# Stores on SP's queue, the output weight split by GpSimd, and another order of column tiles, in a transformer kernel on one core

## The reference

```python
qa, ka, va, ga, qb, kb, vb, gb, qn, kn, vn, gn = split_proj(h @ w_in[l])
lam = (jnp.exp(jnp.sum(lambda_q1[l] * lambda_k1[l])) - jnp.exp(jnp.sum(lambda_q2[l] * lambda_k2[l]))
       + lam_init).astype(jnp.float32)
...
oa = map_query_blocks(lambda q_blk: diff_attend(q_blk, ka_all, va_all, lam), qa)
ya = (rms_norm_2(oa, diff_subln[l]) * (1 - lam_init)).reshape(b, s, A_W) * jax.nn.silu(ga)
...
yb = map_query_blocks(lambda q_blk: gqa_attend(q_blk, kb_all, vb_all), qb) * jax.nn.silu(gb)
...
yn = neighbourhood_attend(qn, kn, vn.reshape(b, s, C_HEADS, HEAD_DIM), kn_c, vn_c, nat_rpb[l], rows)
yn = yn * jax.nn.silu(gn)
y = jnp.concatenate([ya, yb, yn], axis=-1) @ w_out[l]
...
x = x + gt[:, None] * y
```

## Time and profile before

| | us |
|---|---|
| median of three runs | 4307.61 |
| lowest and highest | 4303.0, 4307.77 |
| the profiled execution | 4303.49 |
| its span in the trace | 4301.7 |
| PE busy | 3607.9 (84%) |
| DVE busy | 2565.4 (60%) |
| ACT busy | 2070.9 (48%) |
| GpSimd busy | 1025.2 (24%) |

### The profile page before, as it was taken

How to read it: one execution, slowest core, us unless ns; L and a number is a source line. 1 busy time by engine, 2 the same in 40 slices (tenths; PEclk the granted TensorE clock), 3 DMA queues, 4 the chain that set the end, 5 groups by cost and what they waited for, 6 DMA issues and landing times. The chain is left out here.

```text
span 4301.7 us, 68958 instructions
## 1 busy us (share of the span) xinstructions
PE 3607.9 (84%) x24823; PEld 2975.7 (69%) x24823; DVE 2565.4 (60%) x4482; ACT 2070.9 (48%) x3653; POOL 1025.2 (24%) x964
## 2 busy tenths in 40 slices
PE   3997699988579999589995999974979996999748
PEld 3994487766468888468884778753768875788637
DVE  1205365543677888457645777655558755777654
ACT  1315456751057777542223666654442224766542
POOL 0212100000036656225551000000025560000002
PEclk8998899998689999789997999987989997999989
DMA  7127733313969999433326324431233326244413
GB/s 274 57 85 229 211 79 79 80 38 114 362 255 390 397 396 396 155 141 111 106 76 184 73 59 92 88 64 62 67 134 110 113 79 176 61 91 91 92 47 95
DMA packets 329465, 624.68 MB, mean 145 GB/s; under 512 B 118692, under 2 KB 174916, under 8 KB 328100
## 3 DMA queue, kind: packets, MB, share of 16 engines
q1 hardware_dynamic: 290272, 502.07, 36.7%
q0 software_dynamic: 35040, 104.50, 8.0%
q10 hardware_dynamic: 3812, 13.69, 1.0%
HBM read 486.20 MB, written 133.97 MB: 144 GB/s over the span
## 5 line engine op out<-in xcount | busy, mean ns | idle before, releaser
L1207 ACT ACTIVATE aa_prob<-aa_ps,aa_nm 128x256 f32<-128x256 f32 (+2 forms) x680 | 474.1, 697 | 281.1 <-DVEq L1158 242.5
L1078 PE MATMUL aa_ps<-aa_op 128*128 128x512 f32 (+2 forms) x1408 | 376.4, 381 | 194.8 <-DVEq L1166 126.3
L1157 DVE TENSOR_REDUCE aa_nm<-aa_ps 128x1 f32<-128x1280 f32 (+1 forms) x252 | 346.1, 1373 | 200.7 <-PE aa_ps L1078 188.3
L1078 PEld LDWEIGHTS aa_ps<-aa_op 128*128 128x128 f32 x1408 | 237.2, 194 | 314.9 <-issue 156.2
L1977 PE MATMUL pr_ps<-pr_wH,hT_part 128*128 128x512 f32 (+1 forms) x1120 | 428.7, 383 | 0.0
L1729 ACT ACTIVATE ex_high<-ex_ring 128x2048 fp32r<-128x2048 f32 x192 | 368.7, 1920 | 97.9 <-PE ex_pg L1705 40.1
L1775 DVE TENSOR_TENSOR ex_ring_part<-ex_ring,ex_high 128x2048 fp32r<-128x2048 f32 x144 | 373.8, 2596 | 51.5 <-ACTq L1730 39.8
L1108 PE MATMUL aa_po<-aa_pT,aa_op 128*64 128x128 f32 x5552 | 389.9, 283 | 0.0
L1089 PE MATMUL aa_ps<-ident,aa_prob 128*128 128x128 f32 x2776 | 378.5, 280 | 6.3 <-ACTq L1211 6.2
L1977 PE MATMUL pr_ps<-pr_wH,x_sb_part 128*128 128x512 f32 x896 | 359.4, 401 | 19.9 <-DVEq L2053 19.9
L1977 PE MATMUL pr_ps<-pr_ws_part,x_sb_part 128*128 128x512 f32 x896 | 353.1, 394 | 0.0
(11 more groups left out here) (300 smaller groups left out, 7158.3 us busy)
## 6 DMA issues: line engine op xcount, KB each, us to landing
ex_ring<-in_w_gate SPq DMA_DIRECT2D x64, 1024.0 KB, 10.2
ex_ring<-in_w_up SPq DMA_DIRECT2D x64, 1024.0 KB, 8.7
ex_ring<-in_w_down SPq DMA_DIRECT2D x64, 1024.0 KB, 8.5
aa_op<-z_d SPq DMA_DIRECT2D x120, 320.0 KB, 9.4
z_d<-pr_zT POOLq DMA_DIRECT2D x120, 256.0 KB, 3.1
pr_ws<-in_w_in SPq DMA_DIRECT2D x14, 2048.0 KB, 9.1
mod_w<-in_w_ada SPq DMA_DIRECT2D x10, 2048.0 KB, 13.8
rt_mw<-in_w_ada SPq DMA_DIRECT2D x8, 2048.0 KB, 16.9
```

The source lines that it names most:

```text
L1078: mm = tensor.matmul(ps[:, base[h] + at:base[h] + at + m], q.bitcast(F32R), kk.bitcast(F32R), start=i == 0, stop=i == len(ab) - 1)
L1157: vector.tensor_reduce(most, scores[:, 0:g_.count[t]], AX.X, ALU.max, negate=True)
L1207: scalar.activation(prob[:, base[h] + c0:base[h] + c1], ps[:, base[h] + c0:base[h] + c1], ACT.Exp, bias=nm[:, h % 4:h % 4 + 1], scale=-1.0 ...
```

## The change

Six edits. (1) The attention's output stores go to SP, between its loads; `o` has six buffers instead of four. (2) `w_out` is loaded by SP after the third store; GpSimd makes both of its parts while the last unit runs: the high part goes into the operand slot that the last unit does not use (`operand_slots`), the low part to its old place. `stage_out` makes no parts any more. (3) The lambda vectors are loaded with the near heads' biases, and DVE and ACT make lambda in the attention, from slot 40 on. In `stage_out` SP loads tiles 0 and 1 first, then the gates, for which DVE waits at the third pass only. (4) The projection's stores go to SP, in step order between the weight loads. (5) The output's stores go to SP. (6) The last column tiles are 5, 4, 6 instead of 6, 4, 5: the last one, 6, has no Q or K columns, while 2 now alternates with 5, both with Q and K columns.

```diff
-COLUMN_TILES = (1, 0, 3, 2, 6, 4, 5)
+COLUMN_TILES = (1, 0, 3, 2, 5, 4, 6)
...
+    def operand_slots(held, name, groups):
+        op = held.enter_context(nc.sbuf_tensor(f"{name}_op", [P, 2, max(g_.cols for g_ in groups)], F32))
+        free = sum(g_.pairs for g_ in groups) % 2
+        return op, op[:, free, 0:KC * D].rearrange("p (k d) -> p k d", d=D)
...
+    def stage_attention(name, groups, slots_, weight, asides=(), prepare=None):
+        dv, RING, OR, PREPARE = 64, 4, 6, 40
+        op, wH = slots_
...
+                loads(0)
+                loads(1)
+                for m in range(M):
+                    for u in range(2, len(units)):
+                        if unit_end[u - 2] == m + 1:
+                            sp.wait_ge(pv, m + 1)
+                            loads(u)
+                    g_, p, t, _ = steps[2 * m]
+                    sp.wait_ge(od, m + 1)
+                    sp.dma_start(g_.addr(p)[3][t * P:(t + 1) * P, :], o[:, m % OR]).then_inc(st[m % OR], 16)
+                    if m == 0 and prepare is not None:
+                        prepare[0](sp, extra_ready)
+                    if m == 2:
+                        sp.dma_start(w_sb[:, :, :], w_src.rearrange("(k p) n -> p k n", p=P)).then_inc(w_in, 16)
                         for aside in asides:
                             n_aside += aside(sp, aside_done)
                 if n_aside:
                     sp.wait_ge(aside_done, 16 * n_aside)
+                for b in range(OR):
+                    if len(range(b, M, OR)):
+                        sp.wait_ge(st[b], 16 * len(range(b, M, OR)))
...
-                    if prepare is not None and PREPARE <= s < PREPARE + len(prepare[2]):
+                    if prepare is not None and s - PREPARE in prepare[2]:
...
+                    if prepare is not None and s - PREPARE in prepare[3]:
+                        prepare[3][s - PREPARE](act)
...
-                for m in range(M):
-                    g_, p, t, _ = steps[2 * m]
-                    pool.wait_ge(od, m + 1)
-                    pool.dma_start(g_.addr(p)[3][t * P:(t + 1) * P, :], o[:, m % OR]).then_inc(st[m % OR], 16)
-                for b in range(OR):
-                    if len(range(b, M, OR)):
-                        pool.wait_ge(st[b], 16 * len(range(b, M, OR)))
...
+                pool.wait_ge(w_in, 16)
+                pool.wait_ge(pv, unit_end[-2])
+                for c in range(KC):
+                    pool.tensor_copy(wH[:, c, :].bitcast(F32R), w_sb[:, c, :]).then_inc(w_split, 1)
+                    pool.wait_ge(w_split, 2 * c + 1)
+                    pool.tensor_tensor(w_part[:, c, :].bitcast(F32R), w_sb[:, c, :], wH[:, c, :], ALU.subtract)\
+                        .then_inc(w_split, 1)
+                pool.wait_ge(w_split, 2 * KC)
...
-                if setup:
-                    setup(sp, gl, env)
                 load_tile(sp, 0, tl[0], y_sb, env)
+                load_tile(sp, 1, tl[1], y_sb, env)
                 for m, (row, col) in enumerate(gates):
                     sp.dma_start(g_sb[:, m, :], over_partitions(mod_d[row:row + 1, col:col + D], D)).then_inc(gl, 16)
-                for t in range(1, nt):
-                    if t >= 2:
+                for t in range(2, nt + 4):
+                    if t < nt:
                         sp.wait_ge(t_full, t - 1)
-                    load_tile(sp, t, tl[t % 2], y_sb, env)
-                sp.wait_ge(gl, 16 * (len(gates) + n_setup))
+                        load_tile(sp, t, tl[t % 2], y_sb, env)
+                    if store and t >= 4:
+                        sp.wait_ge(summed, t - 3)
+                        store(sp, t - 4, stored)
+                if store:
+                    sp.wait_ge(stored, 16 * TC * nt)
...
-                        if t == 0:
-                            pe.wait_ge(w_low, c + 1)
...
-                def weights_high(c0, c1):
-                    for c in range(c0, c1):
-                        scalar.activation(wH[:, c, :].bitcast(F32R), w_sb[:, c, :], ACT.Copy)
-                        act.drain().then_inc(w_high, 1)
...
-                def weights_low(c0, c1):
-                    for c in range(c0, c1):
-                        dve.wait_ge(w_high, c + 1)
-                        vector.tensor_tensor(w_part[:, c, :].bitcast(F32R), w_sb[:, c, :], wH[:, c, :], ALU.subtract)
-                        dve.drain().then_inc(w_low, 1)
-                weights_low(0, W0)
-                dve.wait_ge(gl, 16 * (len(gates) + n_setup))
-                if setup_dve:
-                    setup_dve(dve, env)
...
-                    if t == 1:
-                        weights_low(W0, KC)
+                    if t == 2:
+                        dve.wait_ge(gl, 16 * len(gates))
...
-            if store:
-                @block.gpsimd
-                def _(pool):
-                    for t in range(nt):
-                        pool.wait_ge(summed, t + 1)
-                        store(pool, t, stored)
-                    pool.wait_ge(stored, 16 * TC * nt)
...
+                for g in range(len(steps) + LAG):
+                    for i in range(WS, NC):
+                        if end[i - WS] == g:
+                            sp.wait_ge(mm_done, g + 1)
+                            sp.dma_start(w_sb[:, i % WS], wv[:, :, order[i] * N:(order[i] + 1) * N]).then_inc(w_in[i % WS], 16)
+                    if g in raw:
+                        c, t = steps[g]
+                        w = QK[c][0] if c in QK else 0
+                        i = raw.index(g)
+                        sp.wait_ge(ro, i + 1)
+                        c0, c1 = max(w, wanted(c, t)[0]), wanted(c, t)[1]
+                        sp.dma_start(proj2[t * P:(t + 1) * P, c * N + c0:c * N + c1], rb[:, i % RAW, c0:c1]).then_inc(rs[i % RAW], 16)
+                    if g - LAG in qk:
+                        c, t = steps[g - LAG]
+                        q, nm_ = qk.index(g - LAG), QK[c][0] // P
+                        sp.wait_ge(parts, 2 * (q + 1))
+                        for x in (HIGH, LOW):
+                            sp.dma_start(zv[x][:, ZC[c] // P:ZC[c] // P + nm_, t * P:(t + 1) * P], zT[:, q % ZR, x, 0:nm_, :])\
+                                .then_inc(zs[q % ZR], 16)
...
-                    if g in raw:
-                        c, t = steps[g]
-                        w = QK[c][0] if c in QK else 0
-                        i = raw.index(g)
-                        pool.wait_ge(ro, i + 1)
-                        c0, c1 = max(w, wanted(c, t)[0]), wanted(c, t)[1]
-                        pool.dma_start(proj2[t * P:(t + 1) * P, c * N + c0:c * N + c1], rb[:, i % RAW, c0:c1]).then_inc(rs[i % RAW], 16)
...
-                        for x in (HIGH, LOW):
-                            pool.dma_start(zv[x][:, ZC[c] // P:ZC[c] // P + nm_, t * P:(t + 1) * P], zT[:, q % ZR, x, 0:nm_, :])\
-                                .then_inc(zs[q % ZR], 16)
...
+    def differential(held, l):
+        lam0 = 0.8 - 0.6 * math.exp(-0.3 * l)
...
+        def products(dve):
+            vector.tensor_tensor(e["lp"][:, :], e["lv"][:, 0:2 * DK], e["lv"][:, 2 * DK:], ALU.mult)
+            vector.tensor_scalar(e["sg"][:, :], e["sg"][:, :], 1.0 - lam0, None, ALU.mult)
+            dve.drain()
+            vector.tensor_reduce(e["ls"][:, :], e["lp"][:, :].rearrange("p (h d) -> p h d", d=DK), AX.X, ALU.add)
+            dve.drain().then_inc(made, 1)
+        def exponents(act):
+            act.wait_ge(made, 1)
+            scalar.activation(e["le"][:, :], e["ls"][:, :], ACT.Exp)
+            act.drain().then_inc(raised, 1)
+        def difference(dve):
+            dve.wait_ge(raised, 1)
+            vector.tensor_tensor(e["nlam"][:, :], e["le"][:, 1:2], e["le"][:, 0:1], ALU.subtract)
+            dve.drain()
+            vector.tensor_scalar(e["nlam"][:, :], e["nlam"][:, :], lam0, None, ALU.subtract)
+            dve.drain()
+        return e, load, products, exponents, difference
...
+                load_lam(sp, s)
...
+                            prepare=(biases, 7, {0: first_edge, 1: last_edge, 2: inside, 3: products, 6: difference},
+                                     {4: exponents}))
```

More of the change, by code:

```diff
@@ L1044, in _, with loads @@
             def _(sp):
-                n_aside = 0
-                for u in range(len(units)):
-                    if u >= 2:
-                        sp.wait_ge(pv, unit_end[u - 2])
+                def loads(u):
                     for dst, src in itertools.islice(operands(u), 0, None, 1 if u else 2):
@@ L1944, in _ @@
                 sp.dma_start(rot[:, :, :], k["rot"].rearrange("(t p) w -> p t w", p=P)).then_inc(gl, 16)
-                for i in range(WS, NC):
-                    sp.wait_ge(mm_done, end[i - WS] + 1)
-                    sp.dma_start(w_sb[:, i % WS], wv[:, :, order[i] * N:(order[i] + 1) * N]).then_inc(w_in[i % WS], 16)
+                for g in range(len(steps) + LAG):
[17 more added lines that the diff above has]
```

(10 more changed lines are left out.)

100 lines of the change are left out of this document (34 added, 66 removed).

## The result

| | before | after |
|---|---|---|
| median, us | 4305.56 | 4238.91 |
| lowest, highest | 4303.0, 4307.77 | 4236.47, 4241.43 |
| span of the profiled execution | 4301.7 | 4239.6 |
| granted clock | 0.921 | 0.926 |
| DVE busy | 2565.4 | 2504.6 |

The ratio is 0.9845 with a 95% interval of 0.9828 to 0.9863: 66.6 us faster. The forecast was 4270, 4244 to 4294. The sign was right; the gain was nearly twice the forecast, and the time lies 5 us under the range.

The account below looks back on a forecast made before the run. PE, busy 84% of the span, was taken to set the pace of nearly all stages. Terms −24.3 −34.6 −17.0 +9 +30 gave −36.9 us: 4266.6 from the profiled 4303.5, 4270 as a median; range 4244 to 4294.

Parts of the forecast that it names:

- Stage ends: Ends of `am`, `aa0`, `aa1` and the kernel: with SP storing, each gap falls to 2.1 us; −24.3 us together.
- Rival D: Stage ends do not shrink, since GpSimd still has work there: −24.3 falls to about −5; 4297 us, chance 0.05.
- Projection ends: Last projection product to the attention's first load: 3.3 us for 20.6 with tile 6 last; −34.6 us for both layers.
- Starts of the output products: `o20` and `o21`, start to first transposes: 12.7 us instead of 21.9 and 20.5; −17.0 us.
- The split beside DVE: Last unit of `aa0` and `aa1`: DVE's two-SBUF-input operation waits for GpSimd, 0.9 us in five tiles; +9 us.
- rival C: GpSimd's split holds every DVE operation in the last unit of `aa0` and `aa1`: 4324 us, slower; chance 0.03.
- The new order: Projections, column tile 2 beside tile 5: DVE's pairs exceed PE's 11.48 us; +12 in layer 0, +18 in layer 1, +30.
- the upper value: DVE's pair of a tile 2 and a tile 5 step, put at 12.5 to 14.6 us: 14.6 was taken.
- rival A: DVE's pair is cheap, 12.5 us, once the stores leave GpSimd: +7 instead of +30; 4248 us, chance 0.20.
- the lag of three steps: Projection, tile 2 beside 5: slack taken to absorb about 3 of 15.6 us, leaving +12 in layer 0.
- the forecast's 18: Layer 1's share of the new order's cost, where narrower products would have let PE run faster: +18 us.

Follow-up runs that it names:

- The four corners: The changed kernel (4238.9 us), and it with the old column-tile order (4244.3), with the projection's stores on GpSimd (4277.3), with both (4266.6).

## Why the forecast was wrong, step by step

**Stage ends, −24.3.** Measured −5.2, −7.9, −6.6 and −5.4, −25.1. Right; the stage without GpSimd's transfers ends in 1.7 to 2.1 us, and sixteen operations leave a drain of 0.03. Rival D falls: GpSimd's work does not lengthen the end, its transfers do.

**Projection ends, −34.6.** Measured −17.5 and −18.0. Right. The four corners show that it is two edits: 8 us a layer from the stores on SP, 9.5 from the order.

**Starts of the output products, −17.0.** Measured −9.6 and −8.7. Right.

**The split beside DVE, +9.** The mechanism was right, the size too high. DVE's L1159 (L1136 before) and the first near operation of a tile, in `aa1` while GpSimd works, in place of the earlier trace rows:

```profile
4063.23 0.26 DVE L1159 TENSOR_TENSOR aa_den<-aa_den 128x2 f32<-128x2 f32 x1
...
4064.64 0.43 DVE L2348 CUSTOM_DVE_ANT_0 aa_ps<-aa_ps,zeros 128x256 f32<-128x256 f32 x1 [0.27 <-issue]
...
4069.62 0.71 DVE L1159 TENSOR_TENSOR aa_den<-aa_den 128x2 f32<-128x2 f32 x1
...
4071.48 0.43 DVE L2348 CUSTOM_DVE_ANT_0 aa_ps<-aa_ps,zeros 128x256 f32<-128x256 f32 x1 [0.27 <-issue]
```

and GpSimd:

```profile
4069.28 1.04 POOL L1253 CAST aa_op<-w_out 128x1024 fp32r<-128x1024 f32 x1
4070.40 2.35 POOL L1255 TENSOR_TENSOR w_out_part<-w_out,aa_op 128x1024 fp32r<-128x1024 f32 x1
```

L1159 starts at 4069.62 and takes 0.71 us instead of 0.16: until the cast ends (4070.32). The tile takes 6.84 us (4064.64 to 4071.48), not 6.28. Three of these operations wait in `aa0` and four in `aa1`, by 0.10 to 0.58 us and not 0.9. Each meets a cast (1.04 us) and ends with it; none meets a difference (2.36 us). The tiles between them follow each other at 6.84 us, which is two chunks of 3.42, so DVE meets GpSimd at the same place of a chunk again. The tiles beside the split are 2.3 us longer in `aa0` and 2.7 in `aa1` than before, together 5. L2348 (L2350 before), which reads one operand from SBUF and one from PSUM, takes 0.43 as before; rival C falls. Here the Trainium skill, "SBUF — State Buffer", section "Who interferes with whom", says that an operation with one SBUF input outside the 2-port modes is not held; this row agrees.

**The new order, +30.** This is the step that failed. Its working took DVE's 10.8 us in the earlier trace rows as what a step of tile 2 needs, took "the upper value", and put the case in which the stores' move takes the waits away at 0.20, as rival A. The 10.8 are mostly waits for GpSimd's z stores and the difference behind them, and the same change takes those stores away. What the working had computed is a kernel that nobody asked about: the new order with the stores where they were. For that one it was even low: 15.2 us a pair measured against 14.6, 38 to 40 us in the products against 30. In the changed kernel DVE's pair is 11.8 against PE's 11.48, which the lag of three steps takes up in layer 0; the products grow by 1.4 and 1.9 us over the kernel before. GpSimd still holds DVE there, but for less. Beside the rows of DVE above, GpSimd:

```profile
2097.57 0.61 POOL L172 CAST pr_zT<-pr_zT 128x512 fp32r<-128x512 f32 x1 [5.17 <-ACTq L2004]
2098.26 1.30 POOL L174 TENSOR_TENSOR pr_zT<-pr_zT 128x512 fp32r<-128x512 f32 x1
2099.64 1.36 POOL L2125 TENSOR_TENSOR pr_ws_part<-pr_ws,pr_wH 128x512 fp32r<-128x512 f32 x1
```

DVE's L2098 starts at 2098.81, inside the difference L174 (2098.26 to 2099.56), and takes 1.03 us instead of 0.42. Such a wait is mostly 0.3 to 0.6 us in this phase (two of 1.1 us); with an issue ahead of the difference it was 1.2 to 2.7.

**A term that was missing.** With the old order the stores' move shortens layer 1's products from 375.2 to 370.2 us. DVE at 10.8 us a step was over PE's pace with the narrower products there already. In the kernel before PE waits for it at the end of column tile 0's products and at the end of tile 2's:

```profile
3289.78 0.65 PE L1958 MATMUL pr_tp<-ident,pr_z 128*128 128x128 f32 x4 [1.78 <-DVEq L2095]
3300.58 0.66 PE L1958 MATMUL pr_tp<-ident,pr_z 128*128 128x128 f32 x4 [1.78 <-DVEq L2095]
...
3406.78 0.66 PE L1958 MATMUL pr_tp<-ident,pr_z 128*128 128x128 f32 x4 [1.76 <-DVEq L2095]
```

In the old order with the stores on SP none of these waits is left. The forecast's sum had no gain for that, since the earlier trace rows was read only as a bound for the new order and not as a loss that is there. The new order gives it back (379.4): against the old order with the same stores it costs 9.2 us in layer 1, half of the forecast's 18. Of these, 3.9 are a wait of a kind that the forecast did not name, of PE for a weight slice that GpSimd makes late, right behind the pairs of tile 2 and 5:

```profile
3387.41 0.50 PE L1989 MATMUL pr_ps<-pr_wH,x_sb_part 128*128 128x512 f32 x1 [3.89 <-POOL pr_ws_part L2125]
```

The wait of 8.9 us in the run with the stores on GpSimd is of the same kind and is over half of the 15.9 us by which layer 0's products grew there. In the program GpSimd takes a step's slices behind its split of the Q/K step, and that needs DVE's norm and rotation; so DVE's lateness reaches PE by this way too.

With the measured terms the sum is −25.1 − 35.5 − 18.3 + 5 + 3.3 = −70.6, for a measured −66.6. The profiled span moved less, −62.1. Two stretches that the change does not touch took longer in this execution than in that of before: 4.5 us ahead of `am`'s scores and 6.5 from the end of `o1`'s products to layer 0's projection (router and experts). They differ from run to run; a second profiled execution of the same kernel had 1.1 and 2.6 there and a span of 4233.9. Without the two the span moved by −73.1.

One term left at nothing is a loss. From the third on, a token tile of the last output product takes 12.08 us in the changed kernel and in every run with its attention and output stages, also with the split back on ACT and DVE, and 11.80 before; PE is busy all the time in both, at a granted clock of 1.00. The stage's products grow by 3.2 us (107.5 to 110.7). No run shows the cause.

**The range** left out the lower part of A, which the forecast itself put at 4248. A's pair of 12.5 us was too high as well, since it took the 8.7 us of the earlier trace rows, in which L357 and L584 wait for GpSimd too.

## What to carry to other kernels

Before a duration from a trace is added into a new place, ask what it waited for in the old one, and whether the same change takes that away: two edits of one change can be a loss and a gain apart and a larger gain together, so their terms are to be worked out in the state with all the others in. A row whose operation takes longer than the same operation elsewhere (3.54 for four that take 1.43) is a loss to be counted, not only a mechanism. In this kernel transfers that GpSimd issues were paid three times: in the issue, in DVE's operations where a two-input operation of GpSimd stood right behind the issue, and in the drain at the end of the block.
